# Attention in head pairs, last-tile sums joined on TensorE, and the first norm's small steps moved between products

## What is computed

```python
x = layer_norm(x, ln_in_g, ln_in_b)
for l in range(2):
    sh1, sc1, g1, sh2, sc2, g2 = split(silu(c) @ w_ada[l] + b_ada[l], 6)
    z = (x * (1 + sc1) + sh1) @ w_in[l]                 # one input projection, 17 column tiles
    y_a, y_b, y_c, y_d = gating(z), attention(z), s5(z), hgrn2(z)
    x = layer_norm(ALPHA * x + (1 + g1) * (rms_norm(concat(y_a, y_b, y_c, y_d)) @ w_out[l]))
    x = layer_norm(ALPHA * x + (1 + g2) * conv_ffn(x * (1 + sc2) + sh2))
```

## Time and profile before

| what | us |
|---|---|
| median of 3 runs | 1441.2 (1440.73 to 1441.64) |
| the profiled execution's own time | 1442.01 |
| its span on the chip | 1440.1 |
| PE busy | 1357.5 (94%) |
| DVE busy | 775.4 (54%) |
| ACT busy | 510.5 (35%) |
| POOL busy | 542.9 (38%) |
| mean granted TensorE clock | 0.966 of full |

### The profile page before, as it was taken

The page is one execution under the profiler, slowest core; times in us unless marked ns, Lnnn a source line. Parts: engine busy times, 40 slices in busy tenths (PEclk is TensorE's granted clock), DMA queues, the critical chain, the costliest instruction groups (busy, mean ns, idle before and its releaser), DMA issues.

```text
span 1440.1 us, 17110 instructions
## 1 busy us (share of the span) xinstructions
PE 1357.5 (94%) x6812; PEld 1011.1 (70%) x6812; DVE 775.4 (54%) x1370; ACT 510.5 (35%) x778; POOL 542.9 (38%) x328
## 2 busy tenths in 40 slices
PE   5999999999999999899899999999899999989986
PEld 2545676776888888688655577777688888868865
DVE  5885868646676766432468555574533333321135
ACT  2523225335333333322242422343443333332222
POOL 0630100575444444343446010055644444434332
PEclk9999999999999999999999999999899999989998
DMA  9356732032555655454324440102033332323321
GB/s 385 141 117 174 167 117 90 15 102 88 180 200 190 190 175 189 151 199 134 105 84 104 78 79 30 45 16 88 30 113 92 91 100 88 102 61 100 88 73 59
DMA packets 64798, 166.76 MB, mean 116 GB/s; under 512 B 14288, under 2 KB 26960, under 8 KB 64208
## 3 DMA queue, kind: packets, MB, share of 16 engines
q1 hardware_dynamic: 64720, 165.68, 37.7%
HBM read 160.04 MB, written 5.62 MB: 115 GB/s over the span
## 4 chain that ended last, share of the span: by engine, by line
PE 77%; DVE 14%; DMA 3%; issue 2%; SPq 1%; ACT 1%; POOL 1%; POOLq 0%; ACTq 0%; DVEq 0%
PE bank L442 19%; PE bank L444 19%; PE bank L443 19%; PE bank L512 5%; PE bank L506 3%; PE bank L537 2%; PE bank L457 1%; PE bank L683 1%; DVE xa L1012 1%; DVE scr L1201 1%; DVE xa L1018 1%; DMA scr<-in_w_ada 1%; SPq L350 1%; PE bank L665 1%; PE bank L674 1%
## 5 line engine op out<-in xcount | busy, mean ns | idle before, releaser
L2043 POOL TENSOR_TENSOR ring_r<-ring,scr_r 128x1024 fp32r<-128x1024 f32 x148 | 360.0, 2434 | 442.8 <-ACT scr_r L1912 273.4
L442 PE MATMUL bank<-ym_r,scr_r 128*128 128x512 f32 x704 | 280.6, 399 | 5.3 <-DVE hm_r L1564 4.8
L444 PE MATMUL bank<-hm_r,scr_r 128*128 128x512 f32 x704 | 280.1, 398 | 0.0
L443 PE MATMUL bank<-ym_r,ring_r 128*128 128x512 f32 x704 | 277.3, 394 | 0.0
L442 PE MATMUL bank<-scr_r 128*128 128x512 f32 x480 | 196.7, 410 | 28.6 <-issue 14.2
L443 PE MATMUL bank<-scr_r,ring_r 128*128 128x512 f32 x480 | 190.9, 398 | 0.0
L1580 DVE SCALAR_TENSOR_TENSOR scr<-bank,pb,scr 128x511 f32<-128x511 f32 x88 | 66.0, 750 | 212.4 <-ACT scr L1905 212.3
L512 PE MATMUL bank<-hm,ring 128*128 128x512 f32 x352 | 168.5, 620 | 0.0
L1067 DVE SCALAR_TENSOR_TENSOR ada<-ada,silu_c 128x1024 f32<-128x1024 f32 x80 | 134.1, 1679 | 49.6 <-DMA ada<-in_w_ada 49.6
L442 PEld LDWEIGHTS bank<-ym_r,scr_r 128*128 128x128 f32 x704 | 132.8, 189 | 38.3 <-issue 6.4
L444 PEld LDWEIGHTS bank<-hm_r,scr_r 128*128 128x128 f32 x704 | 132.7, 188 | 33.4
(11 more groups left out here) (324 smaller groups left out, 1779.9 us busy)
## 6 DMA issues: line engine op xcount, KB each, us to landing
ring<-in_w_up SPq DMA_DIRECT2D x88, 512.0 KB, 3.6
ada<-in_w_ada SPq DMA_DIRECT2D x80, 512.0 KB, 3.6
ring<-in_w_down SPq DMA_DIRECT2D x44, 512.0 KB, 3.5
ring<-in_w_in SPq DMA_DIRECT2D x34, 512.0 KB, 4.6
scr<-in_w_ada SPq DMA_DIRECT2D x16, 512.0 KB, 14.4
ring<-in_w_out SPq DMA_DIRECT2D x16, 512.0 KB, 3.6
pa<-in_par_a SPq DMA_DIRECT2D x2, 2144.5 KB, 13.1
xa<-in_x SPq DMA_DIRECT2D x1, 2048.0 KB, 8.0
```

Of the source, the lines that this page charges most:

```text
L442: first = mm(dst, w_hi, x_hi, start=start, stop=False)
L443: mm(dst, w_lo, x_hi, start=False, stop=False)
L444: return first, mm(dst, w_hi, x_lo, start=False, stop=stop)
L2043: G.tensor_tensor(ring_r[:, at, :], ring[:, at, :], high[:, at, :].bitcast(F32), ALU.subtract)\
```

## The change

It has four parts.

1. **First norm.** `norm` is cut in three. `norm_var` (5 small instructions) now stands behind the 12th of the 16 modulation products, `norm_rstd` (2 instructions) behind the 13th, `norm_apply` where the norm was.
2. **Last-tile sums** (the four norms inside the layers). DVE and POOL add tiles 0 to 6 only. PE sums these over the partitions, then the last tile of `xa` and its squares in products of their own that accumulate into the same columns: 16 products in place of 8.
3. **Head pairs.** The units go in the order of `block_of`: two heads of a pair at block 0, both at block 1, and so on (widths 128, 128, 256, 256, 384, 384, 512, 512). `values` is done for both heads of a pair at every second step, the two halves in turn, from two buffers (`turned`: `ptt` and the space of `iota`). ACT copies both halves out with one 128x128 instruction, 8 in a layer in place of 16.
4. For that, `steps` is copied once by POOL out of `iota`.

```diff
+def block_of(i):
+    return 2 * (i // 8) + i % 2, (i % 8) // 2
...
+STATS_AFTER = 11
...
+        turned = [ptt, c_f("iota")]
...
+            def norm_sums(tile, col, first, done):
+
+                for b in range(NB):
+                    last = mm(banks[7][:, col + b:col + b + 1], tile[:, b * P:(b + 1) * P], ones[:, 0:1],
+                              start=(first and b == 0), stop=done, skip_group_check=True)
+                return last
+
+            def norm_stats(n, late=None):
+
+                pe.wait_ge(S["ln_sumx"], n)
+                norm_sums(acc[:, 0, :], 64, True, late is None)
+                pe.wait_ge(S["ln_sumq"], n)
+                last = norm_sums(acc[:, 1, :], 68, False, late is None)
+                if late is not None:
+                    pe.wait_ge(S["resid"], (n - 1) * KD)
+                    norm_sums(xa[:, late, :], 64, False, True)
+                    pe.wait_ge(S["ln_sq"], n * KD)
+                    last = norm_sums(hm[:, late, :], 68, False, True)
                 last.then_inc(S["ln_stat"], 1)
...
-                def values(i):
-                    h, b = i // NB, i % NB
-                    pe.wait_ge(S["pt_out"], l * 16 + i + 1)
-                    if i >= 1:
-                        pe.wait_ge(S["pv_out"], l * 16 + i)
+                def values(j):
+                    h, b = block_of(2 * j)
+                    pe.wait_ge(S["pt_out"], l * 16 + 2 * j + 2)
+                    if j >= 1:
+                        pe.wait_ge(S["pv_out"], l * 8 + j)
                     for k in range(b + 1):
-                        last = mm(banks[5][64 * (h % 2):64 * (h % 2) + 64, b * P:(b + 1) * P],
-                                  vb[:, k, h * HD:(h + 1) * HD], ptt[:, k * P:(k + 1) * P],
-                                  start=(k == 0), stop=(k == b))
+                        for hp in range(2):
+                            last = mm(banks[5][64 * hp:64 * hp + 64, b * P:(b + 1) * P],
+                                      vb[:, k, (h + hp) * HD:(h + hp + 1) * HD], turned[hp][:, k * P:(k + 1) * P],
+                                      start=(k == 0), stop=(k == b))
                     last.then_inc(S["pv_mm"], 1)
 
                 def attend(i):
                     if i < 16:
                         scores(i)
-                    if i >= 3:
-                        values(i - 3)
+                    if i >= 4 and i % 2 == 0:
+                        values(i // 2 - 2)
                     if 2 <= i < 18:
                         turn(i - 2)
...
             for i in range(MOD_PRE):
                 modulation(i, mods[:, i:i + 1])
+                if i == STATS_AFTER:
+                    norm_var(1)
+                if i == STATS_AFTER + 1:
+                    norm_rstd(1)
             v.wait_ge(S["ada_used"], MOD_PRE)
             modulated(0, 0)
-            norm(1)
+            norm_apply(1)
...
-                    if i >= 3:
-                        h, b = (i - 3) // NB, (i - 3) % NB
-                        rows = slice(64 * (h % 2), 64 * (h % 2) + 64)
-                        a.wait_ge(S["pv_mm"], l * 16 + i - 2)
-                        A(ym[rows, 2 + h // 2, b * P:(b + 1) * P], banks[5][rows, b * P:(b + 1) * P], ACT.Identity)\
+                    if i >= 4 and i % 2 == 0:
+                        j = i // 2 - 2
+                        h, b = block_of(2 * j)
+                        a.wait_ge(S["pv_mm"], l * 8 + j + 1)
+                        A(ym[:, 2 + h // 2, b * P:(b + 1) * P], banks[5][:, b * P:(b + 1) * P], ACT.Identity)\
                             .then_inc(S["pv_out"], 1)
...
+                        if i >= 4:
+                            a.wait_ge(S["pv_mm"], l * 8 + i // 2 - 1)
...
-                steps = c_f("iota").rearrange("p (o c s) -> p o c s", o=1, s=SC)[:, :, :, 0]
+                steps = steps_t[:, :].rearrange("p (o c) -> p o c", o=1)
+                if l == 0:
+                    ch.link(G.tensor_copy(steps, c_f("iota").rearrange("p (o c s) -> p o c s", o=1, s=SC)[:, :, :, 0]))
```

More of the change, by code:

```diff
@@ L166, in trunk @@
         neg_half = sb("neg_half", [P, 16])
+        steps_t = sb("steps_t", [P, NSC])
         scr, scr_r = twins("scr", [P, SCRATCH])
@@ L656, in scores @@
                 def scores(i):
-                    h, b = i // NB, i % NB
+                    h, b = block_of(i)
                     if i == 0:
@@ L994, in _, with norm_var @@
             ch = Chain(v, S["dve_chain"])
-            def norm(n, low=None):
+            mean, sq, var, rstd, mr = (st[:, 4 * i:4 * i + 4] for i in range(5))
+            def norm_var(n):
                 v.wait_ge(S["ln_stat"], n)
-                mean, sq, var, rstd, mr = (st[:, 4 * i:4 * i + 4] for i in range(5))
                 ch.post(V.tensor_scalar(mean, banks[7][:, 64:68], 1.0 / D, None, ALU.mult))
@@ L1008, in norm, with norm_apply @@
                 V.tensor_tensor(mr, mean, rstd, ALU.mult).then_inc(S["ln_rstd"], 1)
+            def norm_apply(n, low=None):
                 v.wait_ge(S["ln_bcast"], (n - 1) * 2 + 1)
@@ L1023, in norm @@
                         low(k - 3)
+            def norm(n, low=None):
+                norm_var(n)
+                norm_rstd(n)
+                norm_apply(n, low)
             def modulated(l, which):
@@ L1045, in sum_x @@
             def sum_x(done, n, order):
-                if n == 0:
+                if n == 0 or n == KD - 1:
                     return
@@ L1262, in attend @@
                 def attend(i):
-                    b, q = i % NB, i % 2
+                    b, q = block_of(i)[1], i % 2
                     if i < 16:
@@ L1940, in sum_q @@
             def sum_q(norms, order):
-                for n in range(1, KD):
+                for n in range(1, KD - 1):
                     g.wait_ge(S["ln_sq"], norms * KD + n + 1)
```

30 lines of the change are left out of this document (15 added, 15 removed).

## The result

The changed kernel takes 1431.2 us (median of 5 runs, 1424.6 to 1432.0), the kernel before 1441.2 (5 runs, 1439.8 to 1443.6): the ratio over all their runs is 0.9915, 95% interval 0.9893 to 0.9937. By the medians it is faster by 10.0 us, where 12.4 was forecast (1428.8, range 1424.0 to 1435.5). The ratio is lower than that of the two medians (0.9930) and stands for 12.3 us, its interval for 9.1 to 15.4, so the gain is 10 to 12 us and not known more closely. In the last group of experiments the changed kernel took 1429.65 (6 runs, 1423.9 to 1432.9) against 1441.67: ratio 0.9918 (0.9895 to 0.9940), 12.0 us.

A forecast was written before the change was run, and what follows sets the result against it. PE was taken as the bound, 77% of the chain. Gains of 2.6 + 3.3 + 5.2 + 1.3 = 12.4 us from 1442.0 gave 1429.6, less 0.8 for the median 1428.8; own range 1425.5 to 1433.5, full range 1424 to 1435.5.

The forecast's parts named there:

- The first norm: At the start: small steps leave the path behind `modulated` and the 1.98 us wait for spreading goes; gain 2.6 us.
- the five start at 28.5: First norm: the five small DVE steps start at 28.5 us, when PE's partition sums are ready.
- The bound of 2.5 for a slow start: First projection: PE, idle some 3 us, may start at the low clock; priced at nothing, at most 2.5 us lost.
- Head pairs, layer 1: Layer 1 mixers: 16 values blocks, 11.0 us, become 8 pair blocks, 5.9 us; gain 5.2 us.
- Head pairs, layer 0: Layer 0 mixers behind 168.15: ten blocks, 7.3 us, become five, 4.0; gain 3.3. Ahead: nothing, bounds 0.9 gain, 0.5 loss.
- rival b: Layer 0: DVE, with 24 extra products, is as late as PE and the saving becomes waits; 1432.1 us, chance 0.08.
- Sums: Four inner norms: last-tile sums on PE take 19.4 us in place of 20.7; gain 1.3 us.
- a fall at that point leaves some 12 records at the low rate: Inner norms: a clock fall during the 32 one-column records makes them 5.4 us, assumed at two norms of four.
- (a): Inner norms: one-column products keep the clock down, sums take 6.5 to 7.3 us each; 1436 us, chance 0.16.
- (d): All four norms: clock low from the first sum on through later wide products; 7.4 us slower, 1448.6, chance 0.04.
- Rival (e): Inner norms: one-column products take next to nothing, four norms take 7.2 us in place of 20.7; 1416.6, chance 0.01.
- rival c: Pair blocks: the halves don't run side by side, attention gains 1.8 us in place of 8.5; 1435.5, chance 0.05.

The follow-up runs named there:

- c_pairs: The kernel before with only the attention in head pairs, without the first-norm and last-tile-sum parts: 1436.13 us, ratio 0.9955 to the kernel before.
- h_late2: The changed kernel with two idle VectorE products ahead of the first norm's application: 1433.52 us, ratio 0.9945 to the kernel before.
- d_serial: The changed kernel with all products of one head before the other's in each pair block, not in turn: 1431.59 us, ratio 0.9923 to the kernel before.
- e_split: The changed kernel with the 64 thin `s5_kernels` records cut into two halves of 32 around a third of a projection: 1426.32 us, repeated at 1427.28.
- f_early: The changed kernel with the sums of tiles 0 to 6 ahead of the output projection's last weight slice, at two norms: 1433.09 us, ratio 0.9937 to before.
- j_after: The changed kernel unaltered, measured again on one chip beside the split variants: 1429.65 us against 1441.67 for the kernel before, ratio 0.9918.
- g_late1: The changed kernel with one idle VectorE product ahead of the first norm's application: 1430.81 us, ratio 0.9924 to the kernel before.

## Why the prediction came out right, point by point

**The first norm** (forecast 2.6): the mechanism held as described, with products and `modulated` covering the spreading. It gave 2.0 in the profile and 1.8 alone. The step that was too large is "the five start at 28.5": they started at 29.22, since the sums were later. The bound of 2.5 for a slow start was not needed: the clock was low from 39 to 43 (mean 0.57), as I had feared, but the attention still began 2.15 us earlier.

**Head pairs, layer 1** (forecast 5.2): the sizes of the blocks were right to 0.06 us. With the measured sizes the blocks gave 5.4. What I left out are two things that the new order brings. Fewer blocks make the work behind them cheaper: a set of transposes that does not follow a values block costs 0.15 less, and eight in a layer don't any more, 1.2 us. And the narrow scores now come first, ahead of where PE sets the time: steps 3 to 15 have 36 widths of 128 in place of 34, at 0.22 each, 0.4 us more. 5.4 + 1.2 - 0.4 = 6.2, which is what the profiles show, with falls of the clock that cost alike in both (4.47 - 2.77 = 1.7 before, 0.29 + 1.35 = 1.6 after). `c_pairs` fits too: its layer 1 gained 4.6, with falls of 0.83 + 2.48 = 3.3, 1.6 more than before (4.53 for the 64 records and 5.25 for the six behind them). The Trainium skill has the rule, in TensorEngine Tiling (Array Packing), section Key Properties: a change of tiling mode, not just of tile, drains the engine. It gives no price. Going from half-width values to full-width transposes is such a change, and the trace agrees that it costs, 0.15 us each; the drain itself it doesn't show. That the transposes merely lose the cover of a wide product ahead of them is less likely, since L524 pays nothing behind the narrow full-width L563 (1.79) and 0.19 behind the half-width L614 (1.98). No experiment takes the switch by itself.

**Head pairs, layer 0** (forecast 3.3): this is the step that failed in the profile. The sentence "the cover of this part is that PE meets its semaphores in time" was true, and no wait of PE for DVE appeared (rival b is out; the chain behind 168.44 is PE's alone as before). What I had not priced is the clock in the mixers, which I treated as fixed there. Behind 168.44 the mixers were 2.4 us shorter than behind 168.15 before, with 1.65 of excess in them: 4.1 without it, the 3.3 of the forecast and five sets of transposes that are 0.15 cheaper. Ahead of it they were 2.4 longer, with 3.3 of excess; the 0.9 that is left is the forecast's bound for that stretch. So without the four excesses the mixers would have been some 5 us shorter (an estimate, as if each moved the end by its whole length); with them it was 0. `h_late2`, with one fall of 1.6 us in this layer's mixers, took 130.99. Over all profiles the gain is 2.3.

**Sums** (forecast 1.3): they gave 4.0 in the profile and 3.5 alone. I priced a record rightly, 0.131 at full clock; what failed is "a fall at that point leaves some 12 records at the low rate" in two norms of four. The fall came at all four norms, later: only the last eight records were much slower, by 0.4 to 0.8 us a norm, and the first 16, in a row, took 0.115 to 0.12 each. At the full-clock end the estimate said 3.5. Rivals (a) and (d) are out: 16.7 us for the four norms, where (a) needed 26. Rival (e) is out too: eight records behind each other took 1.03 at full clock, 0.13 each. The rule behind it, of the Trainium skill's TensorEngine Tiling (Array Packing), section Instruction Overhead, makes them 0.025 (an estimate from its 60 cycles at 2.4 GHz); the trace does not agree.

**Halves side by side** (rival c): out. `d_serial` takes 1.52 for 16 records where alternating takes 1.03. But the rival was closer than its chance said: alternating itself is worth only 1.5 us a layer, and the rest of the pairs' gain comes with fewer blocks and fewer switches of width, and with what two halves gain without alternating.

**The sum.** Too much for the first norm (0.6) and too little for the sums (2.2 to 2.7) cancelled against the pairs: 8.5 forecast, 6.2 in the profile, 6.1 alone, 7.1 over all profiles. In the profile another 1.9 us were lost outside the changed places, which I had priced at nothing. The result lies in the forecast's own range of 1425.5 to 1433.5, partly by luck: the errors had opposite signs, and single runs of this kernel lie from 4.9 us below the forecast to 4.1 above it (1423.9 to 1432.9).

## What to carry to other kernels

A row of the chain at the same line, with the same count and another length, is the granted clock, and it must be looked up before a gain is called lost or found: here 5 us of one part's gain went this way in one profile and not in others. In a kernel that is 95% PE and is made of narrow products here and there, a change of one or two us per stretch can't be read from one pair of profiles; several variants that share the edit, averaged by stretch, come nearer. And when PE works with halves of its columns, count the switches between half and full width, not the records alone; once that is done, look at the longest row of narrow products that is left, and put wide ones in its middle if the clock falls there: without the pairs it moved the fall and gained nothing.

The version to keep is `e_split`: 1426.3 and 1427.3 us in two measurements, against 1441.1 and 1441.7.

## What the hardware did that I had not expected

- Full-width products cost 0.15 us more behind half-width ones, and it shows up in the row of the full-width ones (0.37 or 0.22 for the same two transposes; 0.19 at L524).
- Two half-width rows for the two halves, one right behind the other, cost some 0.4 us less than their records' price even when they don't alternate (16 records: 1.52; at 0.11 each and 0.14 for the block 1.90; two separate blocks of eight 2.04).
- The clock's falls don't hang on the one row alone. In layer 0 the same 64 records of 16 columns ran at full clock in the kernel before, in `d_serial`, `h_late2` and `f_early`, and with a fall in the changed kernel, in `j_after`'s window of 126 to 137 (mean 0.69), in `c_pairs` and in `g_late1` (both 0.69). In layer 1 they ran at full clock in `j_after` and with a fall in `d_serial`, `h_late2` and `f_early` (4.25, 4.48 and 4.11). Whether something in the pairs' order leads to it, or chance from one execution to the next, was not isolated.
- One program's runs lie as far apart as the whole change: `h_late2` from 1425.56 to 1438.45, and the mean clock goes with it (0.972 and 0.958).
